# Expert turning moved from TensorE to VectorE, five expert pieces loaded at other times, and a last pass by row blocks

## The reference

```python
def moe_swiglu(h, w_router, w_gate, w_up, w_down):
    t = h.reshape(B * S, D)
    logits = (t @ w_router).astype(jnp.float32)
    top_v, top_i = lax.top_k(logits, TOP_K)               # 2 of 8
    top_p = jax.nn.softmax(top_v, axis=-1)
    combine = jnp.sum(jax.nn.one_hot(top_i, N_EXPERTS) * top_p[..., None], axis=1)
    for e in range(N_EXPERTS):
        out = out + combine[:, e:e + 1] * swiglu(t, w_gate[e], w_up[e], w_down[e])
...
return rms_norm(x, final_norm_g)
```

## Time and profile before

| what | value |
|---|---|
| median of 3 runs (lowest to highest) | 1028.89 us (1028.22 to 1030.38) |
| profiled execution | 1027.09 us |
| its span | 1025.3 us |
| busy: TensorE, weight loads, VectorE, ScalarE | 99%, 84%, 51%, 39% |
| chain of waits: TensorE's share | 95% |
| queue of SP: megabytes, share of the 16 DMA engines | 252.94, 66.8% |
| mean granted clock of TensorE | 0.998 |

### The profile page before, as it was taken

How to read it: one execution, slowest core, us unless ns; L and a number is a source line. 1 busy time by engine, 2 the same in 40 slices (tenths; PEclk the granted TensorE clock), 3 DMA queues, 4 the chain that set the end, 5 groups by cost and what they waited for, 6 DMA issues and landing times.

```text
span 1025.3 us, 22421 instructions
## 1 busy us (share of the span) xinstructions
PE 1013.2 (99%) x9857; PEld 856.9 (84%) x9857; DVE 524.0 (51%) x773; ACT 402.0 (39%) x631; POOL 15.7 (2%) x57
## 2 busy tenths in 40 slices
PE   8999999999999999999999999999999999999996
PEld 8999999999999999999999999995646546555553
DVE  6667775687666564476578745854111112112113
ACT  6735656436344353357346654441011002002013
POOL 4000000000000000000000000000000000000000
PEclk9999999999999999999999999999999999999999
DMA  7443543555555475555354348898999999999981
GB/s 283 168 162 104 185 155 114 190 201 179 181 186 187 148 228 184 170 185 184 116 162 157 126 142 328 293 400 347 408 415 415 407 414 415 410 412 413 412 334 42
DMA packets 56016, 255.41 MB, mean 249 GB/s; under 512 B 6609, under 2 KB 6641, under 8 KB 55922
## 3 DMA queue, kind: packets, MB, share of 16 engines
q1 hardware_dynamic: 55346, 252.94, 66.8%
q10 hardware_dynamic: 576, 1.07, 0.3%
HBM read 252.93 MB, written 1.05 MB: 248 GB/s over the span
## 4 chain that ended last, share of the span: by engine, by line
PE 95%; DVE 1%; DMA 1%; ACT 1%; issue 0%; SPq 0%; DVEq 0%
PE ps L1672 35%; PE ps L1667 17%; PE ps L1668 17%; PE ps L1669 17%; PE ps L1661 2%; PE ps L1663 2%; PE ps L1662 2%; DMA raw<-in_dense 1%; PE ps L1877 1%; DVE w_lo L1038 0%; ACT w_hi L714 0%; PE ps L2101 0%; PE ps L2093 0%; PE ps L2084 0%; DVE xhat L1321 0%
## 5 line engine op out<-in xcount | busy, mean ns | idle before, releaser
L1038 DVE TENSOR_TENSOR w_lo<-raw,w_hi 128x1536 fp32r<-128x1536 f32 (+2 forms) x156 | 247.4, 1605 | 119.6 <-ACT w_hi L714 119.3
L714 ACT ACTIVATE w_hi<-raw 128x1536 fp32r<-128x1536 f32 (+2 forms) x156 | 209.2, 1362 | 143.1 <-DMA raw<-in_dense 140.3
L1667 PE MATMUL ps<-hT_hi,w_hi 128*128 128x256 f32 (+1 forms) x816 | 231.7, 284 | 1.8 <-DVE hT_lo L1087 1.1
L1668 PE MATMUL ps<-hT_lo,w_hi 128*128 128x256 f32 (+1 forms) x816 | 230.0, 282 | 0.0
L1669 PE MATMUL ps<-hT_hi,w_lo 128*128 128x256 f32 (+1 forms) x816 | 229.2, 281 | 0.0
L1672 PE MATMUL ps<-e_ring,xe 128*32 128x352 f32 (+2 forms) x2560 | 193.8, 459 | 0.0
L1672 PEld LDWEIGHTS ps<-e_ring,xe 128*32 128x32 f32 x2560 | 113.1, 110 | 74.9 <-issue 34.1
L1667 PEld LDWEIGHTS ps<-hT_hi,w_hi 128*128 128x128 f32 (+1 forms) x816 | 151.9, 186 | 5.5 <-issue 3.5
L1668 PEld LDWEIGHTS ps<-hT_lo,w_hi 128*128 128x128 f32 (+1 forms) x816 | 152.2, 187 | 0.4
L1669 PEld LDWEIGHTS ps<-hT_hi,w_lo 128*128 128x128 f32 (+1 forms) x816 | 152.2, 187 | 0.3
L1672 PE MATMUL ps<-e_ring,ehT 128*32 128x512 f32 (+3 forms) x1144 | 99.4, 495 | 0.0
(11 more groups left out here) (332 smaller groups left out, 1376.6 us busy)
## 6 DMA issues: line engine op xcount, KB each, us to landing
e_ring<-in_experts SPq DMA_DIRECT2D x128, 704.0 KB, 13.7
raw<-in_dense SPq DMA_DIRECT2D x112, 768.0 KB, 4.3
e_ring<-in_experts SPq DMA_DIRECT2D x88, 512.0 KB, 12.3
raw<-in_dense SPq DMA_DIRECT2D x42, 512.0 KB, 3.5
raw<-in_dense SPq DMA_DIRECT2D x3, 544.0 KB, 5.3
raw<-in_dense SPq DMA_DIRECT2D x2, 272.0 KB, 3.9
x<-in_x SPq DMA_DIRECT2D x2, 256.0 KB, 4.5
x<-in_x SPq DMA_DIRECT2D x1, 512.0 KB, 5.9
```

The lines of the kernel that those rows point to most:

```text
L714: act.activation(slot(n, "hi", k), slot(n, "raw", k), ACT.Copy).then_inc(hi_done, 1)
L1038: dve.tensor_tensor(slot(n, "lo", k), slot(n, "raw", k), slot(n, "hi", k).bitcast(F32), ALU.subtract).then_inc(lo_done, 1)
L1667: pe.matmul(out, wh, hi, start=first, stop=False, skip_group_check=True)
L1668: pe.matmul(out, wh, lo, start=False, stop=False, skip_group_check=True)
```

## The change

1. `turn0` and `turn1` are gone from TensorE. VectorE turns `ehid`, `ehid2` and `sel` itself, from SBUF to SBUF, with transposes of 32x32 blocks: 40 instructions and a copy in `turned0`, 24 instructions in `turned1`, each on 32 partitions. `turned1` comes ahead of `select`. TensorE waits for it (`turn1_read`) ahead of block 5 and ahead of the overflow of blocks 4 and 5.
2. Pieces 12, 13 and 14 of the first pass are issued ahead of the two units of `wo` 1 instead of after all branches. Pieces 24 and 25 get a buffer of their own in the first pass, `e_ahead`, and wait for nothing. The scratch of the dynamic queues is set to 4096 bytes. The final gains (`g_row`) are loaded at the start of layer 1.
3. The last pass does both column halves and the overflow block by block like the others. At block 10 the overflow comes first. Then the overflow's products, the high, the low and the f32 ones of half 1 (from `ehid`, without a low part) are placed, and the sums and squares go by two halves.

```diff
-LAST_BANKS = ((2, 3), (0, 1), (5, 7))
+LAST_BANKS = ((2, 3), (0, 1))
...
-LAST_CUT = HALF + 384
-NORM_PIECES = [[], [], [], OCOLS, [(0, HALF), (HALF, LAST_CUT - HALF), (LAST_CUT, D - LAST_CUT)]]
+NORM_PIECES = [[], [], [], OCOLS, [(0, HALF), (HALF, HALF)]]
...
+def branch_banks(l, i):
+
+    return Y_BANKS * l + sum((OCOLS[j % 3][1] // P + 1) // 2 for j in range(3, i + 1))
...
-E_FREE_LATER = (((0, 1, 2, 3, 4, 5, 16, 17), "v"), ((6, 7, 8, 9, 10, 11, 12, 13, 14, 15), "y"), ((18, 19), "wo"),
+E_STAGED = ((12, ("wo", 1), 0, 4), (13, ("wo", 1), 0, 4), (14, ("wo", 1), 1, 6))
+E_FREE_LATER = (((0, 1, 2, 3, 4, 5, 16, 17), "v"), ((6, 7, 8, 9, 10, 11, 15), "y"), ((18, 19), "wo"),
                 ((20, 21), "router"), ((22, 23), "counts"))
 
 
+AHEAD = (24, 25)
...
+        e_ahead = sb("e_ahead", [len(AHEAD) * 2 * HALF_E])
...
-        def e_unit(u):
+        def e_unit(u, first=False):
 
             _, _, _, k, _, c = E_UNITS[u]
             at, size = e_place(u)
-            return e_ring[:, at:at + size].rearrange("p (k c) -> p k c", k=k)
+            place = e_ring[:, at:at + size]
+            if first and u in AHEAD:
+                place = e_ahead[:, AHEAD.index(u) * size:(AHEAD.index(u) + 1) * size]
+            return place.rearrange("p (k c) -> p k c", k=k)
...
-            def expert_load(u, experts):
+            def expert_load(u, experts, first=False):
                 which, e, k0, k, c0, c = E_UNITS[u]
                 src = block_of(t["experts"][experts[e]], expert_at[which, k0, k, c0, c], k, c)
-                sp.dma_start(e_unit(u), src).then_inc(loaded_e[u // 2], 16)
+                sp.dma_start(e_unit(u, first), src).then_inc(loaded_e[u // 2], 16)
...
+                for u, step, kh, branch in E_STAGED:
+                    if n == FIRST[1, step][0] + kh:
+                        sp.wait_ge(y_ready, branch_banks(1, branch))
+                        expert_load(u, (0, 1))
...
             for u in range(24, len(E_UNITS)):
-                sp.wait_ge(e_used, E_GROUP[e_before(u)] + 1)
-                expert_load(u, (0, 1))
+                if u not in AHEAD:
+                    sp.wait_ge(e_used, E_GROUP[e_before(u)] + 1)
+                expert_load(u, (0, 1), first=True)
...
+                if l:
+                    act.dma_start(g_row[:, :], t["final_norm_g"].partition_broadcast(P)).then_inc(s_grow, 16)
...
             act.wait_ge(y_filled, last * 2 + 1)
+            weighted_over()
+            act.wait_ge(y_filled, last * 2 + 2)
             weighted(0)
-            act.wait_ge(y_filled, last * 2 + 2)
-            weighted_over()
-            for tt in range(TT):
-                act.wait_ge(x_sum, tt + 1)
-                squares(0, tt, 4)
             act.wait_ge(y_filled, last * 2 + 3)
-            w = LAST_CUT - HALF
-            act.activation(y_hi[:, HALF:LAST_CUT], ps[:, 6, 0:w], ACT.Copy, scale=slot_scale[:, 0:1]).then_inc(y_hi_ready, 1)
-            for piece in (1, 2):
+            act.activation(ehid[:, 0:HALF], ps[:, 6, :], ACT.Copy, scale=slot_scale[:, 0:1]).then_inc(y_hi_ready, 1)
+            for h in range(2):
                 for tt in range(TT):
-                    act.wait_ge(x_sum, TT * piece + tt + 1)
-                    squares(piece, tt, 4)
+                    act.wait_ge(x_sum, TT * h + tt + 1)
+                    squares(h, tt, 4)
...
+            quadrants = [slice(OV * a, OV * (a + 1)) for a in range(4)]
+            slots_of = ehid[:, :].rearrange("p (k c) -> p k c", c=P)
+            over_of = ehid2[:, :].rearrange("p (k c) -> p k c", c=P)
+
+            def turn_main(k0, k1):
+
+                for a in quadrants:
+                    for b in quadrants:
+                        ins = dve.transpose(ehT[a, k0:k1, b], slots_of[b, k0:k1, a])
+                return ins
+
+            def turn_over(k, b, at, n, quarters=range(4)):
+
+                for a in quarters:
+                    ins = dve.transpose(ehT2[quadrants[a], k:k + n, :], over_of[quadrants[b], at:at + n, quadrants[a]])
+                return ins
+
+            def turn_sel(i):
+
+                to = ehT[:, TURNED:TURNED + 2 * TT, :]
+                of = sel[:, :, :].bitcast(F32).rearrange("p t (part s) -> p (t part) s", part=2)
+                for a in quadrants:
+                    for b in quadrants:
+                        ins = dve.transpose(to[a, :, b], of[b, :, a])
+                ins.then_inc(turn0_read, 1)
+                dve.wait_ge(turn0_read, i * 3 + 2)
+                dve.tensor_copy(selT[:, :, :].rearrange("s part (t c) -> s t part c", t=TT),
+                                to.rearrange("s (t part) c -> s t part c", part=2)).then_inc(turn0_read, 1)
+
             def turned0(i):
 
-                dve.wait_ge(turn0_filled, i * 3 + 1)
-                dve.tensor_copy(ehT[:, 0:4, :], ps[:, 5, :].rearrange("p (a b) -> p a b", b=P)).then_inc(turn0_read, 1)
-                dve.wait_ge(turn0_filled, i * 3 + 2)
...
-                dve.wait_ge(turn0_filled, i * 3 + 3)
-                dve.tensor_copy(selT[:, :, :], ps[:, 7, :].rearrange("p (a b) -> p a b", a=2)).then_inc(turn0_read, 1)
+                dve.wait_ge(hid_ready, i * 6 + 3)
+                turn_main(0, TURNED)
+                turn_over(0, 0, 0, 3)
+                turn_over(3, 1, 0, 3, (0, 1))
+                turn_over(3, 1, 0, 2, (2, 3)).then_inc(turn0_read, 1)
+                turn_sel(i)
 
             def turned1(i):
 
-                dve.wait_ge(turn1_filled, i * 2 + 1)
-                dve.tensor_copy(ehT[:, 5:9, :], ps[:, 0, :].rearrange("p (a b) -> p a b", b=P)).then_inc(turn1_read, 1)
-                dve.wait_ge(turn1_filled, i * 2 + 2)
...
-                dve.tensor_copy(ehT[:, 9:11, :], ps[:, 1, 0:2 * P].rearrange("p (a b) -> p a b", b=P)).then_inc(turn1_read, 1)
...
                 hidden(i, 1)
+                turned1(i)
                 select(lambda n, w: pslots[:, :, bass.ds(i * 2 + 2 + n, w)])
-                turned1(i)
...
-            dve.wait_ge(y_hi_ready, last * 4 + 1)
+            for h in range(2):
+                dve.wait_ge(y_hi_ready, last * 4 + h + 1)
+                ins = rest_over(h)
+            ins.then_inc(y_split, 1)
+            dve.wait_ge(y_hi_ready, last * 4 + 3)
             rest(0)
             for h in range(2):
-                dve.wait_ge(y_hi_ready, last * 4 + h + 2)
-                ins = rest_over(h)
-            ins.then_inc(y_split, 1)
-            def last_rows(piece):
-
-                c0, w = NORM_PIECES[4][piece]
                 for tt in range(TT):
-                    dve.wait_ge(added_filled, last * 4 + 4 + 2 * piece + tt + 1)
-                    xs_ = x[:, tt, c0:c0 + w]
-                    dve.tensor_tensor(xs_, ps[:, LAST_BANKS[piece][tt], 0:w], xs_, ALU.add).then_inc(x_sum, 1)
-
-            last_rows(0)
-            dve.wait_ge(y_hi_ready, last * 4 + 4)
-            rest(1, LAST_CUT - HALF)
-            last_rows(1)
-            dve.wait_ge(y_filled, last * 2 + 4)
-            dve.tensor_scalar(ehid[:, 0:D - LAST_CUT], ps[:, 4, 0:D - LAST_CUT], slot_scale[:, 0:1], None, ALU.mult).then_inc(last_ready, 1)
-            last_rows(2)
+                    dve.wait_ge(added_filled, last * 4 + 4 + 2 * h + tt + 1)
+                    xs_ = x[:, tt, h * HALF:(h + 1) * HALF]
+                    dve.tensor_tensor(xs_, ps[:, LAST_BANKS[h][tt], :], xs_, ALU.add).then_inc(x_sum, 1)
...
+                    if k == TURNED:
+                        pe.wait_ge(turn1_read, i * 2 + 1)
                     for h in range(2):
                         down_main(k, h)
+                if q == TURNED // 2:
+                    pe.wait_ge(turn1_read, i * 2 + 2)
                 down_over(k_pair(q)).then_inc(e_used, 1)
...
-            def second_half(i):
-
-                hidden(1, 0, i)
-                turn0(i)
-                hidden(1, 1, i)
-                hidden(1, 2, i)
-                hidden(1, 3, i)
+            def second_half(i, first=False):
+
+                for q in range(KQ):
+                    hidden(1, q, i, first)
+                pe.wait_ge(scale_ready, i + 1)
+                pe.wait_ge(added, i * 4 + 4)
                 pe.wait_ge(turn0_read, i * 3 + 3)
...
-                second_half(i)
-                down(0, i)
-                turn1(i)
-                down(1, i)
-                pe.wait_ge(turn1_read, i * 2 + 4)
-                for q in range(2, DQ):
+                second_half(i, first)
+                for q in range(DQ):
...
             second_half(last)
-            for k in range(4):
-                down_ready(k, last)
-                down_main(k, 0)
-            turn1(last)
-            w = LAST_CUT - HALF
-            for k in range(4):
-                down_main(k, 1, w=w)
-            pe.wait_ge(turn1_read, last * 2 + 4)
-            for k in range(4, FET):
-                down_ready(k, last)
-                down_main(k, 0)
-            for q in range(DQ):
-                ins = down_over(k_pair(q))
```

(72 more changed lines are left out.)

51 lines of the change are left out of this document (5 added, 46 removed).

## The result

| | before | after |
|---|---|---|
| median (lowest to highest) | 1029.62 us (1028.22 to 1030.38, 4 runs) | 1017.78 us (1017.30 to 1019.16, 4 runs) |
| profiled execution | 1027.09 us | 1018.14 us |
| its span | 1025.3 us | 1016.4 us |
| last expert load lands | 999.48 | 1000.18 |
| from there to the end | 25.8 us | 16.2 us |

The ratio of the medians is 0.9889, with a 95% interval of 0.9875 to 0.9903: the change makes the kernel 11.8 us faster. The forecast was 1017.8 us, 11.1 us less. In a later group of runs the same two kernels are 10.8 us apart (1028.45 and 1017.61).

The account below looks back on a forecast made before the run. TensorE bound the kernel, expert loads close behind; after the change loads end last. Last landing 998.4 plus tail 15.8 gives span 1014.2, 11.1 us less; with 1.8 around the span and 1.8 to the median, 1017.8 us, range 1014.5 to 1022.

Parts of the forecast that it names:

- What binds: Whole expert stream: TensorE ends last before, loads close behind; after the change loads end last, by 2.2 us.
- Part 1, turning: Expert passes: removing TensorE's transposes saves 3.4 us a pass, 12.1 us up to the last down projection; VectorE's work is covered.
- an estimate of 13.1 us for turned0: VectorE's turned0: at the skill page's 311 ns for each transpose it would take 13.1 us, still covered by 19.4 free.
- Part 2, staged loads: Expert load queue: staging pieces 12 to 14 gives 0; the buffer for 24 and 25 lands the last load 1.1 us earlier.
- the two stretches as described: Load queue: 652 to 664, at 207 GB/s, has room for staged pieces; the queue then goes idle earlier, before 682.
- a sign against it: w_o stretch: waits of TensorE there would show the prediction wrong; rival of staging hurting this stretch, 1020.8 us, 5%.
- the forecast 1.1: Last expert landing: the piece issued at 704.0 lands at 708.7 instead of 709.8, moving the last landing from 999.5 to 998.4.
- the whole stream behind piece 28 keeps the gain: Loads behind the piece issued at 704.0: all come 1.1 us earlier, nothing is starved after, backlog grows to 16 us.
- Part 3, the tail: End of the last pass: 15.8 us from the last landing to the end, against 25.8 before.
- a sign that the prediction gives for being wrong: Last down projection: a landing in the chain that is not the one starting the last block; no size given.
- The sum: Whole kernel: landing 998.4 plus tail 15.8 gives span 1014.2, 11.1 us less; profiled 1016.0, median 1017.8 us.

Follow-up runs that it names:

- experiment 4: Changed kernel loading only the first half of each down piece from the second pass on, all TensorE instructions kept (half_down): 1016.08 us, ratio 0.9870.
- experiments 1 and 4: 1: kernel before with VectorE turning alone (turn_only, 1030.15 us) or the new last pass alone (tail_only, 1028.28 us); 4: changed kernel with half down loads (half_down, 1016.08 us).
- half_down: Changed kernel loading only the first half of each down piece from the second pass on, stale weights in the rest: 1016.08 us, ratio 0.9870.
- no_stage: Changed kernel with pieces 12 to 14 issued after all branches again, 24 and 25 keeping their buffer: 1017.36 us, ratio 0.9893.
- turn_only: Kernel before with the turning on VectorE alone, its loads and last pass as they were: 1030.15 us, ratio 1.0004.
- ahead28: Changed kernel with the own buffer given to pieces 28 and 29 instead of 24 and 25, issued first: 1017.15 us, ratio 0.9890.
- tail_only: Kernel before with the new last pass alone, turning on TensorE and the old loads: 1028.28 us, ratio 0.9994.
- loads_only: Kernel before with part 2 (staged and early loads) alone: 1028.24 us, ratio 0.9989.
- after_again: Changed kernel unaltered, run again for comparison on the same chip: 1017.61 us, ratio 0.9898.
- turned1_late: Changed kernel with 12 more VectorE transposes of 32x192, into scratch, ahead of turned1: 1021.94 us, ratio 0.9933.

## Why the prediction was right, point by point

**What binds.** Right. The loads land at one pace whatever TensorE does: from the last piece of the first pass to the last of the fourth, 255.3 us before and 255.1 after, 85.1 us a pass (forecast from 412 GB/s: 84.0). The waits for loads were forecast as several and some 2 us; they are six, and cost 2.0 us by experiment 4. The last landing stays within 1.3 us (307.82 to 309.06) whether TensorE's pass takes 81.65 or 78.30 us, as long as pieces 24 and 25 lie in the ring, and experiments 1 and 4 show both sides of it.

**Part 1, turning.** The pass is 78.30 us (742.80, 821.10, 899.40 on VectorE), 3.35 less than before against 3.4. A transpose of 32 rows takes 235 ns at 64 columns and 370 ns at 192, so about 168 ns and 1.05 ns a column; I had 0.25 to 0.35 us. turned0 took 13.3 us (forecast 12.1) and turned1 8.3 us (7.6). VectorE: DVE Perf Modes (the Trainium skill), The three transpose paths, has 311 ns for a 128x128 transpose by 32x32 blocks in bf16, which I took for each instruction in an estimate of 13.1 us for turned0. The trace agrees in size: 235 to 370 ns for one instruction of 32 partitions in f32. The advice of the same page (Rules for kernel authors) to give a 128x128 transpose to TensorE doesn't hold here, where VectorE had 19 us free and TensorE none. No pass waited for turned blocks before the loads did; one wait in the last pass, 0.95 us of a weight load, is named after VectorE's overflow transposes (L1569), but these had ended at 986.90, 0.7 us before it ended (987.61); it stands one step of 5.05 us, the time of four pieces, ahead of the waits for loads at 992.66 and 997.71; half_down, where only the loads differ, hasn't it; and the second piece of block 5 lands at 987.50, 0.1 us before the wait ends. It was a wait for a load.

**Part 2, staged loads.** The staging is worth 0, as forecast, by a trace with the two stretches as described and by no_stage. One wait in the w_o stretch stood at 1.21 us (662.85, on VectorE's split `hT_lo`), which the prediction had named as a sign against it. It isn't one: turn_only, which stages nothing, has it with 1.03 us (of before none is as long), and ahead28, which does, hasn't one over 0.4 us.

The last landing moved from 307.82 to 306.88 from the first use, 0.94 us for the forecast 1.1, but that the size fits is partly luck, for it is the sum of two effects of which I had one. Turning on VectorE without the buffer makes the landing later (308.45 to 309.06 against 307.82 and 308.16 for before and tail_only), and the buffer then brings it 1.9 us forward. In loads_only, where TensorE turns as before, piece 28 lands 1.5 us earlier than before (16.58 for 18.06, and 16.52 in the changed kernel), yet the last landing is at 307.95: there nothing of it reached the end. That the whole stream behind piece 28 keeps the gain, as the forecast had it, is therefore not shown in general.

In the three kernels that turn on VectorE without the buffer piece 26 was issued 7.9 to 8.5 us after the first use and not 7.1, and piece 28, issued at the same 12.3, landed 6.7 us later instead of 5.8. What delays piece 26 stays open.

**Part 3, the tail.** The new end is a landing and a tail of 16.2 us; forecast 15.8. ScalarE starts 0.82 us after the last landing (0.6), VectorE's remainders end at 3.8 (3.5), its sums at 8.4 (8.15), the last square at 9.15 (9.0), and 7.05 us follow (6.8). The first of these has a reason that I had missed, and a sign that the prediction gives for being wrong, a landing in the chain that isn't the one that starts the last block, did come up: block 9's landing, 2.5 us earlier, sets when block 10 starts as much as its own does, for TensorE needs 1.7 us for the block and 0.9 for the pair's overflow. It costs some 0.2 us and leaves the mechanism as it was: two pieces land every 2.5 us, and TensorE meets them at block after block and not in one wait at the last.

**The sum.** 1016.4 for the span against 1014.2: 1.6 of the 2.2 us are the later first use, 0.4 the tail and 0.2 the landing. In after_again, with its first use at 692.00, the span was 1015.0. Both profiled times, 1018.14 and 1016.80, are 1.8 us above their spans, as taken. The profiled time came out 2.1 us above the 1016.0 of the forecast. The median still meets the forecast, because that adds another 1.8 us, by which the median of before lay above its profiled execution, and in the changed kernel's runs the median lies 0.4 us below it. The mechanism held, and the terms of the sum came out within 0.5 us; that the median agrees to 0.1 us is luck.

## What to carry to other kernels

When two resources are within a few per cent of each other, work out for each when it would end alone, and from the later one what must still follow it. A change that speeds up the other one, or that shortens the work behind the earlier one, gives nothing alone; the two together gave 11 us here. Measure the distance by taking half of one resource's work away. A wait in the rows of the weight loads overstates what TensorE loses: 4.2 us there were 2.0 us of time, and in turn_only 18.8 us there were 9.9 in the rows of the matmuls.

## What the runs showed of the hardware

- A VectorE transpose of 32 partitions in f32 took 235, 269, 303, 336 and 370 ns at 64, 96, 128, 160 and 192 columns, in steps of 33 to 34 ns for each further 32x32 block. With 192 columns into the scratch of turned1_late it took 341 ns in the mean, and 12 in a row 3.60 us; into `ehT` 370 ns, and 16 in a row 6.12 us. What makes the difference is open.
- The stream of loads kept a pace of 84.9 to 85.2 us for the 54 pieces of a pass in all three intervals of before and of after, while the first use of an expert piece moved by 1.3 us between two executions of one kernel (693.30 and 692.00), and with it the span.
- The weight loads of TensorE stood still 0.9 us longer than its matmuls did: waits for a landing that ended at 992.66 and at 997.71 were 1.45 us each in the rows of the weight loads and 0.54 in those of the matmuls.
- In turn_only, where TensorE stood longest in front of its loads, its granted clock went from 1.00 to 0.50 behind a stretch with 4.80 us of work in 10, and was 0.50 from 999.5 to 1005.5.
